# A second stage with twenty chunks instead of twenty-four, and the last four projected inside the delta block

## The chip, the core and the metric

The kernel runs on one NeuronCore of one Trainium2 chip. The time is that of the device for one execution of the program, in microseconds (us). Five engines work side by side, each through its own list of instructions in order: TensorE (PE), VectorE (DVE), ScalarE (ACT), GpSimd (POOL) and SyncE (SP, which here only issues DMAs). They wait for each other through semaphores that the kernel sets by hand. All data is 32-bit floating point. A matmul of that type is recorded twice in the profile, so a group "x2" of one shape is one matmul.

## The reference

One transformer trunk layer over 128 context tokens and 512 latent tokens: layer norm with a modulation, a token mixer of three recurrences (a gated delta rule, a linear recurrent unit, an mLSTM), each gated and projected, and a mixture of experts. What the change touches is cut down here to its core:

```python
def token_mixer(h, p, init_state):
    proj = h @ p['w_in']
    qkv_a, x_b, z_a, beta_a, alpha_a, g_b, q_c, k_c, v_c, o_c, i_c, f_c, gates = _split(proj, IN_SIZES)
    y_a, st_a = delta_mixer(silu(dwconv(qkv_a, p['conv_a'])), z_a, beta_a, alpha_a, ...)
    y_b, st_b = lru_mixer(dwconv(x_b, p['conv_b_w']) + p['conv_b_b'], g_b, p, s_lru)   # (h_f + h_b) * gelu(g_b)
    y_c, st_c = mlstm_mixer(q_c, k_c, v_c, o_c, i_c, f_c, ...)

def gated_delta_chunked(q, k, v, g, beta, s0):          # chunks of 128 tokens, here 5 tiles
    kk = einsum('bnhid,bnhjd->bnhij', kc, kc)
    strict_l = where(strict, bc[..., :, None] * kk * decay, 0.0)
    sol = triangular_solve(eye + strict_l, rhs, left_side=True, lower=True)
    ...                                                  # then a scan over the tiles, forward and backward
    o = rms_norm(o_f + o_b, norm_w) * silu(z)
```

q and k are divided by their norms over the 128 channels of a head before all this. The mod vectors (shift, scale and gate of both halves of the layer) are `silu(c) @ w_mod + b_mod`.

## The kernel before

The program is a row of blocks, each with a list for every engine and a barrier at its end. Two of them are touched.

**`proj1` (lines 400 to 680).** The hidden activations lie transposed in `hT` (8 slices of 128 channels by 640 tokens). The input weights come from memory in ten blocks of 2 MB through `ring`, which holds two. A block has four chunks of 128 output columns; a chunk is 8 slices of one 128x512 and one 128x128 matmul (L464, L465). First come 40 matmuls of 32 columns for the small projections (L442), then 24 chunks in six blocks: the input of the recurrent unit (0 to 3), its gate `g_b` (4 to 7), the delta rule's q, k and v (8 to 19) and its gate z (20 to 23). After each chunk PE does a third of one mod vector: half of its row (L169, `mod_half`, twice), or the turning of a finished row into columns (L176), for which DVE must first have copied the row from `bank[7]` (L654). ACT and DVE take each chunk out of PSUM; chunks of the first and third to fifth block go through a convolution of four steps on DVE (L601 or L608, and L611 three times). Beside chunks 8 to 15 run the gates of the recurrent unit, its two directions are scanned on DVE in one piece each, ahead of chunk 12 and ahead of chunk 16 (`direction`, L643), and GpSimd computes the inner part of gelu after that (L550 to L554). At the end DVE multiplies it out (L675, L677).

**`delta` (lines 798 to 1395).** v and k are turned to tokens by channels (L894, L914), squares (POOL, L1222) are summed by a matmul with ones (L904), ACT makes 1/norm as Ln and Exp (L1141, L1146), DVE multiplies q and k by it (L1262). For each of the five tiles PE forms k k^T (L929) and the decay rows (L920), DVE and ACT make the triangular matrix N (L1275, L1154, L1288). Its 32x32 diagonal blocks go to memory (L807, four DMAs a tile) and come back with one block per partition (L812), where DVE inverts all 80 at once, row by row (L1300, L1303, some 35 us). They go back to memory (L817) and come into place tile by tile (`load_inverse`, 12 DMAs, L831 and L835, which need buffers that POOL has zeroed, L1238). From them PE builds each tile's whole inverse in four products (`inner` L947, `inner_product` L956, `turned` L963, `outer` L971, `outer_product` L980), and a loop of five steps g carries the two directions' states on (L920, L1010, L1017, L1024, L1031, L1037, L1044). Between these PE does projections for the mLSTM, q, k and v, one slice (an eighth of a unit) at a time; the table `FILL` says how many at which place. Then come the four units of the mLSTM's output gate (L1063, `gate_unit`), the sums of squares for the final norm (L1074) and the turning of the mLSTM's k (L1090).

The order of everything is written out by hand: the lists `lab_*` and `l*` number the semaphore steps, and a wait names the step that it wants.

## Time and profile before

| | us |
|---|---|
| time, median of 3 runs (lowest to highest) | 1605.72 (1603.92 to 1609.12) |
| time of the profiled execution | 1603.87 |
| its span from first to last instruction | 1601.9 |
| PE busy | 1364.6 (85% of the span) |
| DVE busy | 579.8 (36%) |
| ACT busy | 279.7 (17%) |
| POOL busy | 106.9 (7%) |
| mean granted TensorE clock | 0.926 of full speed |

The profile is of one execution; 2.0 us of its time lie outside the span. "Idle before" names what ended a wait. A clock of 1.00 is 2.4 GHz, one of 0.50 is 1.2 GHz; a value between them in a stretch is a mixture of the two. `proj1` lasts from 44 to 344 us, the delta block from 344 to 691 us.

### The profile page before, as it was taken

What the parts mean: (1) busy time and instruction counts of PE and PEld (TensorE: products, weight loads), DVE (VectorE), ACT (ScalarE), POOL (GpSimd) and SP (SyncE); (2) the same over time, 40 slices, a digit from 0 to 9 for tenths busy, and PEclk for the clock granted to TensorE, in tenths of its full rate; (3) what the DMA queues carried; (4) which work ended last, traced back from release to release, by engine and by line L of the source; (5) the groups of instructions that cost most, each with busy time, mean ns of one, the idle gap of its engine ahead of it and who ended that gap; (6) DMA issues with size and microseconds to landing.
All of it is one profiled execution on the core that took longest, in us unless ns stands there. A gap on an engine that the chain in (4) does not pass through costs nothing. (4 is left out here: it accounts for less than half of the span.)

```text
span 1601.9 us, 16015 instructions
## 1 busy us (share of the span) xinstructions
PE 1364.6 (85%) x6201; PEld 805.5 (50%) x6201; DVE 579.8 (36%) x1294; ACT 279.7 (17%) x574; POOL 106.9 (7%) x150
## 2 busy tenths in 40 slices
PE   4999995978967999899999999999948888786864
PEld 2655553555635889466777555554543333232321
DVE  4231568223381345244444411115751111110108
ACT  2102441034102433211111100000111101110110
POOL 0000003011000000000000000002011111110100
PEclk9799997989987999999999999999958999998987
DMA  9332322310301101022111127103068999999923
GB/s 374 145 131 106 105 76 82 130 55 1 82 14 32 34 6 58 0 80 66 40 40 40 40 79 246 63 20 141 40 284 325 421 424 423 424 423 373 391 85 151
DMA packets 57742, 242.36 MB, mean 151 GB/s; under 512 B 21668, under 2 KB 30436, under 8 KB 42820
## 3 DMA queue, kind: packets, MB, share of 16 engines
q1 hardware_dynamic: 51476, 229.79, 37.3%
q0 software_dynamic: 6048, 10.50, 1.7%
q8 instruction: 50, 0.82, 0.2%
q10 hardware_dynamic: 144, 1.05, 0.2%
q14 instruction: 24, 0.20, 0.0%
HBM read 233.54 MB, written 19.31 MB: 158 GB/s over the span
## 5 line engine op out<-in xcount | busy, mean ns | idle before, releaser
L464 PE MATMUL bank<-hT,ring 128*128 128x512 f32 x384 | 202.5, 609 | 0.0
L2431 PE MATMUL bank<-ew,xgT 128*64 128x512 f32 x672 | 162.8, 640 | 35.0 <-DMA ew<-in_experts 18.4
L1531 PE MATMUL bank<-hT,w_ab 128*128 128x512 f32 x256 | 131.1, 594 | 0.8 <-issue 0.8
L2431 PEld LDWEIGHTS bank<-ew,xgT 128*64 128x64 f32 x672 | 57.6, 148 | 136.0 <-issue 136.0
L465 PEld LDWEIGHTS bank<-hT,ring 128*128 128x128 f32 x384 | 74.2, 193 | 94.4 <-issue 94.4
L2445 PE MATMUL bank<-ew,hidT 128*64 128x512 f32 x336 | 80.1, 619 | 12.8 <-issue 12.3
L1532 PEld LDWEIGHTS bank<-hT,w_ab 128*128 128x128 f32 x256 | 48.6, 190 | 61.2 <-issue 61.2
L2540 DVE SCALAR_TENSOR_TENSOR uh<-uh,bank 128x256 f32<-128x256 f32 x21 | 8.8, 421 | 191.6 <-ACT uh L2494 191.6
L465 PE MATMUL bank<-hT,ring 128*128 128x128 f32 x384 | 74.6, 276 | 0.0
L1942 PE MATMUL bank<-w_out,mT 128*128 128x512 f32 x160 | 70.9, 604 | 2.2 <-PEq L1464 2.2
L867 PE MATMUL bank<-hT,ring 128*128 128x512 f32 x128 | 66.0, 597 | 0.0
L1646 PE MATMUL bank<-hT,w_c 128*128 128x512 f32 x128 | 65.5, 594 | 0.0
L464 PEld LDWEIGHTS bank<-hT,ring 128*128 128x128 f32 x384 | 59.4, 195 | 9.2 <-issue 3.4
L2445 PEld LDWEIGHTS bank<-ew,hidT 128*64 128x64 f32 x336 | 27.5, 141 | 51.9 <-issue 51.9
L1942 PEld LDWEIGHTS bank<-w_out,mT 128*128 128x128 f32 x160 | 30.8, 194 | 40.3 <-issue 40.3
L1532 PE MATMUL bank<-hT,w_ab 128*128 128x128 f32 x256 | 49.2, 274 | 0.0
L2551 DVE COPY yo<-bank 128x512 f32<-128x512 f32 x21 | 14.5, 692 | 95.3 <-PE bank L2445 95.3
L2494 ACT ACTIVATE uh<-bank 128x256 f32<-128x256 f32 x21 | 8.1, 384 | 184.7 <-PE bank L2431 184.7
L868 PEld LDWEIGHTS bank<-hT,ring 128*128 128x128 f32 x128 | 24.4, 190 | 30.9 <-issue 30.9
L1647 PEld LDWEIGHTS bank<-hT,w_c 128*128 128x128 f32 x128 | 24.3, 190 | 30.6 <-issue 30.6
L1063 PE MATMUL bank<-hT,ring 128*128 128x512 f32 x64 | 34.9, 629 | 5.4 <-ACT og L1215 5.4
L611 DVE SCALAR_TENSOR_TENSOR yc_half<-rawc,cah,yc_half 128x642 f32<-128x642 f32 x36 | 39.1, 1085 | 1.3
(427 smaller groups left out, 2102.6 us busy)
## 6 DMA issues: line engine op xcount, KB each, us to landing
ew<-in_experts SPq DMA_DIRECT2D x41, 2048.0 KB, 20.8
ew<-in_experts SPq DMA_DIRECT2D x41, 1024.0 KB, 22.5
ring<-in_blocks SPq DMA_DIRECT2D x10, 2048.0 KB, 9.5
mhalf<-in_mods SPq DMA_DIRECT2D x16, 1024.0 KB, 5.0
w_ab<-in_merge SPq DMA_DIRECT2D x16, 768.0 KB, 4.4
mstage<-in_mods SPq DMA_DIRECT2D x3, 2048.0 KB, 18.6
w_c<-in_merge SPq DMA_DIRECT2D x8, 768.0 KB, 4.4
yt<-expert_rows SPq DMA_DIRECT2D x5, 1024.0 KB, 9.0
```

What stands on the lines that cost most here:

```text
L464: pe.matmul(lat[:, :], w, hT[:, k, P:T], start=(k == 0), stop=(k == KD - 1))
L465: mm = pe.matmul(ctx[:, 0:P], w, hT[:, k, 0:P], start=(k == 0), stop=(k == KD - 1))
L611: dve.scalar_tensor_tensor(dst, rawc[:, s_, j:j + CW], w[j], dst, ALU.mult, ALU.add).then_inc(v1.step("conv", c, j), 1)
L867: pe.matmul(lat[:, :], w, hT[:, k, P:T], start=(k == 0), stop=(k == KD - 1))
L868: mm = pe.matmul(ctx[:, 0:P], w, hT[:, k, 0:P], start=(k == 0), stop=(k == KD - 1))
L1063: pe.matmul(lat[:, :], w, hT[:, k, P:T], start=(k == 0), stop=(k == KD - 1))
L1531: pe.matmul(bank[5][:, :], w[:, k, :], hT[:, k, P:T], start=(k == 0), stop=(k == KD - 1))
L1532: mm = pe.matmul(bank[7][:, 0:P], w[:, k, :], hT[:, k, 0:P], start=(k == 0), stop=(k == KD - 1))
L1646: pe.matmul(bank[4 * s_][:, :], w_c[x][:, k, :], hT[:, k, P:T], start=(k == 0), stop=(k == KD - 1))
L1942: mm = pe.matmul(bank[2 * (t % 2) + f][:, :], mT[k // 4][:, k % 4, tok(t)], w_out[:, k, 512 * f:512 * f + 512], start=(k == 0), stop=(k == ...
L2431: mm = pe.matmul(bank[2 + x % 2][hs, :], xgT[:, x % 2, k, hs], ew1[:, 2 * (x % 2) + h, 2 * DE * k:2 * DE * (k + 1)], start=(k == 0), stop= ...
L2445: mm = pe.matmul(bank[5 + f][HS * h:HS * h + HS, :], hidT[:, x % 2, P * k + HS * h:P * k + HS * h + HS], ew2[:, 2 * (x % 2) + h, at:at + 5 ...
```

## The change

`proj1` has 20 chunks; the z gate's four become units at the end of the `DENSE` list in the delta block, and their weight block is the ninth to be loaded, not the sixth. The mod work of the four missing chunks is done in chunks 16 to 19, two thirds of a vector each, one of them in the middle of the chunk's sum. Their halves come through two buffers, and ACT, not DVE, copies the last three rows. The scans of a direction are spread, one channel group per chunk (12 to 15 and 16 to 19). The small projections are computed with tokens as columns (16 matmuls) and turned by five transposes after chunk 0. gelu moves to the delta block, to ACT and DVE; GpSimd does none of it. The delta block starts with the keys' norms, whose squares ACT makes at the end of `proj1`; the queries' norms and the turning of v and k come after the five tiles' matrices. The SP queue waits for q's fourth unit only after the blocks are read back, and reads them with two DMAs, not ten. In the loop the decay rows and the key-state product of step g + 1 stand within the building of its inverse.

```diff
-    C1 = 24
+    C1 = 20
+    MOD = {c: ([c] if c < 16 else [2 * c - 16, 2 * c - 15]) for c in range(C1)}
...
-            for t in range(NT):
-                for k in range(KD):
-                    mm = pe.matmul(bank[6][:, 32 * t:32 * t + 32], hT[:, k, tok(t)], w_small[:, k, :],
-                                   start=(k == 0), stop=(k == KD - 1))
+            for k in range(KD):
+                pe.matmul(bank[6][0:32, :], w_small[:, k, :], hT[:, k, P:T], start=(k == 0), stop=(k == KD - 1))
+                mm = pe.matmul(bank[7][0:32, 0:P], w_small[:, k, :], hT[:, k, 0:P], start=(k == 0), stop=(k == KD - 1))
             mm.then_inc(p1.step("small", 0), 1)
...
+                if m < 9:
+                    pe.wait_ge(v1.sem, v1.after("row", m))
+                else:
+                    pe.wait_ge(a1.sem, a1.after("row", m))
+                    if m > 9:
+                        pe.wait_ge(v1.sem, v1.after("column", m - 1))
+                    else:
+                        pe.wait_ge(a1.sem, a1.after("tg1", 7))
+                mod_columns(pe, bank[7 if m < 9 else 6][:, 0:8], mrow[:]).then_inc(p1.step("columns", m), 1)
+            for m in range(5):
...
+                        if k == 3 and len(MOD[c]) == 2:
+                            mod_step(MOD[c][0])
...
+            act.wait_ge(p1.sem, p1.after("small", 0))
+            act.activation(tr[0:32, P:T], bank[6][0:32, :], ACT.Copy).then_inc(a1.step("st", 0), 1)
...
+                if c in (16, 18, 19):
+                    m = {16: 9, 18: 10, 19: 11}[c]
+                    act.wait_ge(used, 2 * (m - 4) + 2)
+                    act.wait_ge(p1.sem, p1.after("columns", m - 1))
+                    act.activation(mrow[:], bank[7][:, :], ACT.Copy).then_inc(a1.step("row", m), 1)
...
-                if c in (12, 16):
-                    direction(0 if c == 12 else 1)
-                if c % 3 == 2:
+                if c % 3 == 2 and c < 16:
                     mod_row(4 + c // 3)
+                if 12 <= c < 20:
+                    scan((c - 12) // 4, c % 4)
                 chunk(c)
-                if c % 3 == 2:
-                    mod_column(4 + c // 3)
+                for i in MOD[c]:
+                    if i % 3 == 2:
+                        mod_column(4 + i // 3)
...
+    DENSE = [("q", j) for j in range(4)] + [("k", j) for j in range(4)] + [("v", t) for t in range(NT)] + [("z", j) for j in range(4)]
+    FILL = {("prep", 1): 8, **{("head", t): 1 for t in range(NT)}, ("sub",): 53}
+    FILL.update({("l0", x): 3 for x in range(4)})
+    FILL.update({("a", 0): 8, ("b", 0): 8, ("c", 0): 10, ("a", 1): 0, ("b", 1): 0, ("c", 1): 8})
+    FILL.update({("a", 2): 4, ("b", 2): 4, ("c", 2): 8, ("a", 3): 4, ("b", 3): 4, ("c", 3): 0, ("a", 4): 0, ("b", 4): 0, ("c", 4): 0})
...
+    lp = [("gcs",)] + [("sum", i) for i in KEYS]
     for t in range(NT):
-        lp += [("kk", t), ("gb", t, 0), ("gb", t, 1)]
+        lp += [("gb", t, 0), ("gb", t, 1), ("kk", t)]
+    lp += [("sum", i) for i in QUERIES] + [(x, t) for x in ("v", "k") for t in range(NT)]
...
-    FILL = {("prep", 0): 4, **{("sum", i): 1 for i in NORMS}, ("prep", 1): 8, **{("head", t): 2 for t in range(NT)}, ("sub",): 46}
-    FILL.update({("l0", x): 3 for x in range(4)})
-    for g in range(NT):
-        FILL.update({(x, g): 2 if g < 2 else 1 for x in "abc"})
-    FILL[("rest",)] = 8 * len(DENSE)
...
-            sp.wait_ge(pd.sem, pd.after("q", 3))
-            load_block(sp, 8)
             for t in range(NT):
                 sp.wait_ge(v3.sem, v3.after("N", t, 1))
...
             sp.wait_ge(n_sent, 16 * 4 * NT)
-            for t in range(NT):
-                for d in range(2):
-                    sp.dma_start((xt if d else xb)[16 * t:16 * t + 16, d, :, :].rearrange("p i j -> p (i j)"),
-                                 n_dram[t, d].rearrange("h r i j -> (h r) (i j)")).then_inc(got_n, 16)
+            for d in range(2):
+                sp.dma_start((xt if d else xb)[0:NB, d, :, :].rearrange("p i j -> p (i j)"),
+                             n_dram[:, d].rearrange("t h r i j -> t (h r) (i j)")).then_inc(got_n, 16)
+            sp.wait_ge(pd.sem, pd.after("q", 3))
+            load_block(sp, 7)
             sp.wait_ge(v3.sem, v3.after("xt"))
             for d in range(2):
                 for dst, src in ((x_dram, xb), (xt_dram, xt)):
...
-            for g in range(2, NT):
+            load_inverse(2)
+            sp.wait_ge(pd.sem, pd.after("v", NT - 1))
+            sp.dma_start(ring[:, 0, :], A["blocks"][8]).then_inc(got_z, 16)
+            for g in range(3, NT):
                 load_inverse(g)
-            sp.wait_ge(pd.sem, pd.after("v", NT - 1))
+            sp.wait_ge(pd.sem, pd.after("z", 3))
             sp.dma_start(ring[:, 0, :], A["blocks"][9]).then_inc(got_o, 16)
...
+                    if kind == "z":
+                        if j:
+                            pe.wait_ge(v3.sem, v3.after("sil", j - 1))
+                        else:
+                            pe.wait_ge(got_z, 16)
+                            pe.wait_ge(ad.sem, ad.after("v", NT - 1))
...
             for t in range(NT):
+                for d in range(2):
+                    if t:
+                        pe.wait_ge(v3.sem, v3.after("A", t - 1, d))
+                    else:
+                        pe.wait_ge(a3.sem, a3.after("ln", KEYS[3], d))
+                    decay_rows(o_bank(d), t, d).then_inc(p3.step("gb", t, d), 1)
+                if t == 0:
+                    fill("prep", 1)
+                    pe.wait_ge(v3.sem, v3.after("norm", 7))
                 if t >= 2:
                     pe.wait_ge(v3.sem, v3.after("N", t - 2, 1))
-                else:
                 for h in range(H):
                     mm = pe.matmul(hd(bank[4 + t % 2], h), kt(t, h), kt(t, h), start=True, stop=True)
                 mm.then_inc(p3.step("kk", t), 1)
-                for d in range(2):
-                    if t:
-                        pe.wait_ge(v3.sem, v3.after("A", t - 1, d))
-                    decay_rows(o_bank(d), t, d).then_inc(p3.step("gb", t, d), 1)
                 fill("head", t)
+            for m, i in enumerate(QUERIES):
+                pe.wait_ge(a3.sem, a3.after("square", i))
+                if m < 2:
+                    pe.wait_ge(v3.sem, v3.after("N", NT - 1, 1))
+                else:
+                    pe.wait_ge(a3.sem, a3.after("ln", QUERIES[m - 2], 1))
+                square_sums(m, i)
+
+            def turn(x, t):
+                for h in range(H):
+                    src = qkv[:, 8 + h, ctok(t)] if x == "v" else kt(t, h)
+                    mm = pe.transpose(bank[4 + t % 4][:, P * h:P * h + P], src, ident)
+                mm.then_inc(p3.step(x, t), 1)
...
             fill("sub")
+            for t in range(NT):
+                if t < 4:
+                    pe.wait_ge(a3.sem, a3.after("v", t if t else 4))
+                else:
+                    pe.wait_ge(a3.sem, a3.after("k", 0))
+                turn("k", t)
...
+            inner(0)
+            fill("l0", 0)
+            inner_product(0)
+            fill("l0", 1)
+            turned(0)
+            gates(0)
+            fill("l0", 2)
+            outer(0)
+            key_state(0)
+            fill("l0", 3)
+            outer_product(0)
+            for g in range(NT):
+                more = g + 1 < NT
+                for d in range(2):
+
+                    if d:
+                        fill("a", g)
...
                 if more:
                     turned(g + 1)
+                    gates(g + 1)
                     outer(g + 1)
+                    key_state(g + 1)
                     outer_product(g + 1)
...
             gate_unit(0)
-            for t in (0, 2, 3):
+            for t in DONE:
                 square_sum(t)
             gate_unit(1)
-            for t in (1, 4):
-                square_sum(t)
             gate_unit(2)
...
+                        dve.wait_ge(ad.sem, ad.after("z", j))
+                        dve.scalar_tensor_tensor(yA[:, j, P:T], yA[:, j, P:T], 1.0, bank[0][:, :], ALU.add, ALU.mult)
+                        dve.scalar_tensor_tensor(yA[:, j, 0:P], yA[:, j, 0:P], 1.0, bank[1][:, 0:P], ALU.add, ALU.mult).then_inc(v3.step("sil", j), 1)
...
                 if more:
+                    weighted(g + 1)
                     put_outer(g + 1)
+                silu_z("c", g)
```

On PE, at the start of the delta block, the rows of before are these, up to the first tile's k k^T (L929) and decay rows (L920); L867 and L868 are slices of the mLSTM's projection and L904 is the sum of squares.

```order
L886 MATMUL bank<-smg,cst 128x20 x2
L887 MATMUL bank<-smg,cst 128x40
L894 MATMUL bank<-cst,qkv 128x128 x20
...
L904 MATMUL bank<-sq,cst 128x321 x2
...
L914 MATMUL bank<-cst,qkv 128x128 x20
L929 MATMUL bank<-qkv 128x128 x4
L920 MATMUL bank<-cst,smg 128x128 x8
```

And now (L951 is the sum of squares, L964 the decay rows, L928 and L929 a slice, L980 is k k^T):

```order
L947 MATMUL bank<-smg,cst 128x20 x2
L948 MATMUL bank<-smg,cst 128x40
L951 MATMUL bank<-xc,cst 128x321 x8
L964 MATMUL bank<-cst,smg 128x128 x8
L928 MATMUL bank<-hT,ring 128x512
L929 MATMUL bank<-hT,ring 128x128
...
L980 MATMUL bank<-qkv 128x128 x4
```

The transposes of v and k have left the place ahead of the first tile, and of sixteen matmuls of squares eight are left there; one whole unit of eight slices stands between, where there were twenty slices.

On the SP queue, before, from the delta block's start to the return of the inverses (L156 is a load of a weight block):

```order
L156 DMA ring<-in_blocks 128x4096
L807 DMA delta_n_blocks<-dl_n 32x8x32 x20
L812 DMA dl_x<-delta_n_blocks 16x1024
L812 DMA dl_xt<-delta_n_blocks 16x1024
...
L817 DMA delta_x_blocks<-dl_x 80x1024
```

And now:

```order
L855 DMA delta_n_blocks<-dl_n 32x8x32 x20
L859 DMA dl_x<-delta_n_blocks 80x1x1024
L859 DMA dl_xt<-delta_n_blocks 80x1x1024
L156 DMA ring<-in_blocks 128x4096
L866 DMA delta_x_blocks<-dl_x 80x1024
```

The twenty sends no longer stand behind the load of a weight block, which waits for PE's fourth unit; the load now stands behind the two reads.

On PE, the second step of the loop, before, from the products that complete its inverse (L980) to the next tile's first product (L947):

```order
L980 MATMUL bank<-dl_f,dl_d_1687 128x64 x4
L980 MATMUL bank<-dl_f,dl_d_1688 128x64 x4
L920 MATMUL bank<-cst,smg 128x128 x8
L1010 MATMUL bank<-dl_s_1685,qkv 128x128 x4
L1010 MATMUL bank<-dl_s_1686,qkv 128x128 x4
L1017 MATMUL bank<-qkv 128x128 x8
L863 MATMUL bank<-ring,hT 128x512 x2
L1024 MATMUL bank<-dl_w_1661,dl_dt_1674 128x128 x4
L1024 MATMUL bank<-dl_w_1662,dl_dt_1675 128x128 x4
L947 MATMUL bank<-dl_dt_1672,dl_n 128x64 x4
```

And now, with L1053 for L980, L964 for L920, L1076 for L1010, L1098 for L1017, L1104 for L1024 and L1020 for L947:

```order
L964 MATMUL bank<-cst,smg 128x128 x8
L1044 MATMUL bank<-dl_dt_1564,dl_n 128x64 x4
L1044 MATMUL bank<-dl_dt_1565,dl_n 128x64 x4
L1076 MATMUL bank<-dl_s_1575,qkv 128x128 x4
L1076 MATMUL bank<-dl_s_1576,qkv 128x128 x4
L1053 MATMUL bank<-dl_f,dl_d_1577 128x64 x4
L1053 MATMUL bank<-dl_f,dl_d_1578 128x64 x4
L1098 MATMUL bank<-qkv 128x128 x8
L1104 MATMUL bank<-dl_w_1551,dl_dt_1564 128x128 x4
L1104 MATMUL bank<-dl_w_1552,dl_dt_1565 128x128 x4
L1020 MATMUL bank<-dl_dt_1562,dl_n 128x64 x4
```

The decay rows and the key-state product have moved ahead of L1053, and no slices are left between it and L1020.

## Rows read from the trace of the kernel before

**Rows 1.** Windows: stretch, its us, busy (x) per engine, PEclk, DMA share, GB/s.
```profile
44.00:691.00 647.00, 573.29 (x2716) 377.70 (x2716) 266.84 (x540) 167.55 (x315) 35.55 (x31) 0.91 0.19 65
...
44.00:61.00 17.00, 16.75 (x81) 16.78 (x81) 1.32 (x4) 1.49 (x2) 0.00 (x0) 0.52 0.63 248
...
272.00:281.00 9.00, 8.40 (x22) 5.21 (x23) 4.86 (x8) 0.74 (x1) 0.00 (x0) 0.55 0.00 0
...
492.00:499.00 7.00, 7.00 (x21) 5.00 (x22) 0.00 (x0) 0.60 (x1) 0.00 (x0) 0.53 0.01 2
...
800.00:1000.00 200.00, 199.21 (x909) 125.50 (x908) 71.56 (x235) 22.49 (x57) 0.00 (x0) 1.00 0.27 87
```

**Rows 2.** PE's timeline, its longest waits: start, us, line [idle before, releaser].
```profile
272.60 1.87 PE L176 MATMUL bank<-cst,mrow 128*128 128x2 f32 x8 [17.52 <-DVE mrow L654]
...
344.07 1.02 PE L886 MATMUL bank<-smg,cst 128*128 128x20 f32 x4 [8.27 <-PEq L414]
...
491.89 3.68 PE L947 MATMUL bank<-dl_dt,dl_n 128*128 128x64 f32 x16 [26.21 <-DMA dl_d<-delta_xt_blocks]
...
667.77 2.08 PE L1063 MATMUL bank<-hT,ring 128*128 128x512 f32 x2 [5.44 <-ACT og L1215]
```

**Rows 3.** PE's timeline, small projections, then two neighbouring slices and a mod half.
```profile
44.25 16.91 PE L442 MATMUL bank<-w_small,hT 128*128 128x32 f32 x80 [3.15 <-PEq L212]
...
67.42 1.02 PE L464 MATMUL bank<-hT,ring 128*128 128x512 f32 x2
...
68.50 1.02 PE L464 MATMUL bank<-hT,ring 128*128 128x512 f32 x2
...
71.84 1.06 PE L169 MATMUL bank<-mhalf,cond 128*32 128x512 f32 x8
```

**Rows 4.** DVE's timeline: one convolution step beside GpSimd's gelu, and without.
```profile
256.00 4.42 DVE L608 TENSOR_SCALAR yc_half<-rawc,cah 128x642 f32<-128x642 f32 x1
...
272.78 0.55 DVE L608 TENSOR_SCALAR yc_half<-rawc,cah 128x642 f32<-128x642 f32 x1
```

**Rows 5.** SP's timeline at the end of `proj1`.
```profile
335.05 0.33 SPq L156 DMA_DIRECT2D ring<-in_blocks  x1
335.50 0.35 SPq L163 DMA_DIRECT2D out_lru<-nlru  x1
```

**Rows 6.** SP's waits over the first 800 us: total, times, longest.
```profile
SPq L414 <- DMA out_lru<-nlru: 7.2, 1, 7.2
```

**Rows 7.** DVE's timeline: last matrix N, first and last step of the inversion.
```profile
419.72 2.15 DVE L1288 SCALAR_TENSOR_TENSOR dl_n<-bank,dl_nb,dl_w 128x128 f32<-128x128 f32 x8
442.85 1.04 DVE L1293 COPY dl_x<-dl_xt 80x1024 f32<-80x1024 f32 x1 [20.97 <-DMA dl_xt<-delta_n_blocks]
...
476.28 2.06 DVE L1307 COPY dl_xt<-dl_x 80x2048 f32<-80x2048 f32 x1
```

**Rows 8.** SP's timeline: the sends of N, and the first inverse's loads.
```profile
421.17 13.57 SPq L807 DMA_DIRECT2D delta_n_blocks<-dl_n  x20
...
484.89 1.74 SPq L831 DMA_DIRECT2D dl_dt<-delta_xt_blocks  x4
```

**Rows 9.** ACT's timeline in the delta block: a whole-gate tanh, a table switch, eight Exps.
```profile
344.05 2.34 ACT L1132 ACTIVATE dl_tz<-yA 128x2560 f32<-128x2560 f32 x1 [6.17 <-PEq L414]
...
370.77 1.28 ACT L1146 ACT_TABLE_LOAD   x1
372.07 5.13 ACT L1146 ACTIVATE rs<-rs 128x642 f32<-128x642 f32 x8
```

**Rows 10.** POOL's timeline, zeroing ahead of the second inverse's loads.
```profile
513.73 0.99 POOL L1238 MEMSET dl_d<- 128x512 f32 x2 [56.84 <-PE bank L980]
```

**Rows 11.** PE's timeline in the loop.
```profile
511.78 1.90 PE L980 MATMUL bank<-dl_f,dl_d 128*128 128x64 f32 x16
...
522.84 2.00 PE L947 MATMUL bank<-dl_dt,dl_n 128*128 128x64 f32 x16 [0.25 <-DMA dl_d<-delta_xt_blocks]
...
539.37 3.47 PE L980 MATMUL bank<-dl_f,dl_d 128*128 128x64 f32 x16 [0.78 <-ACT dl_f L1161]
...
638.52 1.95 PE L1044 MATMUL bank<-dl_qk,dl_u 128*128 128x128 f32 x16
```

390 lines of the change are left out of this document (212 added, 178 removed).

## The prediction, made before the changed kernel had run

> **What bounds the kernel now.** I read the windows first. From 44 to 691 us, the two blocks that change, PE is busy 573.3 of 647 us at a mean granted clock of 0.91, while DVE has 267 us of work and ACT 168 [rows 1]. PE is the only engine that is nearly full, so time goes here in three ways: its work, its idle time (73.7 us), and work done at the low clock. That PE work alone need not slow the clock is seen from 800 to 1000 us, 99.6% busy at 1.00 [rows 1]. The second view is PE's timeline, for the waits. Four make 57.4 us of the 73.7: 17.5 us for DVE's copy of a mod row, 8.3 us at the barrier ahead of the delta block, 26.2 us for the inverse's blocks from memory, and 5.4 us for ACT in the gate units [rows 2]. After each long wait come 4 to 9 us at the low clock: 272 to 281 us at 0.55, 492 to 499 us at 0.53 [rows 1]. Third, the timelines of DVE, ACT, POOL and SP, for what each wait hangs on.
>
> The units of the sum: a slice is 68.50 - 67.42 = 1.08 us, a chunk of eight 8.65, a third of a mod vector about 1.0 [rows 3]. A group of 16 matmuls of 128 or 64 columns in the loop takes some 1.8 us to the next one; 1.9 is recorded [rows 11]. Slices of v have no 128-column part and take 0.87. Below, D is the start of the delta block on PE, 344.07 before [rows 2].
>
> **Small projections.** 16.9 us for 80 records from 44.25 [rows 3], all at the low clock (0.52 with PE busy 16.75 of 17 us [rows 1]): PE had been idle before. Now it is eight pairs of 512 and 128 columns. If their first 4 us are slow, as in the other restarts, that is two pairs of 2.17, six of 1.08, chunk 0 at 8.65 and transposes of 1: 20.5 us, to 64.8. Before, the same point was 71.8, where the first mod half starts [rows 3]. I take -7. Bounds: if the clock stays low until chunk 0, as before, eight pairs of 2.17, two slow slices, six fast ones and the transposes make 29, +1.5; if it never falls, 18.3, -9.
>
> **Scans spread, gelu away from POOL.** Before, DVE does a whole direction ahead of chunk 16's work, then a convolution beside GpSimd: one step takes 4.42 us, which takes 0.55 without it [rows 4]. So the mod row is late and PE waits 17.5. Now a DVE turn is at most a product of 2.8, two scans (1.7), a chunk's convolution (3.6) and a gate's three operations (1.9), near 11 us against a PE turn of 11.9. The wait goes, with the slow 9 us behind it, which did 8.4 x 0.55 = 4.6 us of work in 8.4: -17.5 - 3.8 = -21.3. What is late next: the row copy on ACT at chunk 18. ACT's queue ahead of it is chunk 17's copy, its tanh (after DVE's convolution, some 5 us after the chunk), and two squares of 0.75. That is 7.6 us after chunk 17's end; PE wants it 1 + 4.3 = 5.3 after. +2.4 (bounds 0 and +5).
>
> **Four chunks leave.** -34.6 at this place. They come back below, slice for slice. Mod work is the same.
>
> **The barrier.** DVE's gelu tail goes, but SP loads a block at 335.05, stores the states at 335.50 and waits 7.2 us for them [rows 5, 6]. That stays: PE's wait of 8.3 becomes about 7.5. -0.8. So D comes at 344.1 - 7 - 21.3 + 2.4 - 34.6 - 0.8 = 282.8.
>
> **From D to the first product with an inverse** (491.89 - 344.07 = 147.8 before [rows 2]). Now: sums of the keys' squares, Ln and Exp take 16 us on ACT and DVE, under PE's first unit; the first k k^T is at D + 19. Each tile then costs DVE 4.3 us (two groups of 2.15 [rows 7]) and PE 4.1. N is done at D + 41.6, where it was 421.9 - 344.07 = 77.8 [rows 7]. The sends, 13.57 us for 20, all came after N because SP waited for PE's fourth unit [rows 8]; now four remain, 2.7 us. The merged reads are not in this trace. From the last send, 434.7, to DVE's first step on the blocks, 442.85, it was 8.1 us with five pairs [rows 7, 8]; I take 5, bounds 2 and 12, and they are hidden: DVE is busy with gelu (three operations of 2.8) until D + 52.7, 3 us longer. The inversion takes 35.5 us [rows 7] and comes free at D + 88.
>
> But PE is not there. After the last tile it waits for N (4 us), for ACT between the second and third query sum (3 us: ACT first does gelu's square and tanh, 2.34 each [rows 9]), and for v's first copy; these pieces run at the low clock. The 53 slices begin at D + 60.2, and their first 4 us are slow. POOL zeroes its buffers only after k's last unit, 51 slices on: 60.2 + 2.2 + 55.3 = 117.7; 1.5 for three memsets of 0.5 [rows 10]; then SP's loads, 7.0 from issue to PE's first product (491.89 - 484.89 [rows 2, 8]). The first product is at D + 126. PE's own work reaches it at D + 124.6, so a wait of 26.2 has become 1.6. This rests on PE; the inversion has 28 us in hand.
>
> The switches of ACT's tables stand on this path twice more (Ln, then Exp, for the queries). The trace has 1.28 us from a switch to the first Exp at 372.07, 1.30 after its start [rows 9], and this is in the sum. The Trainium skill (ScalarE: Activation LUTs, "What ACT_TABLE_LOAD costs") adds a drain, 2.66 us in all; by that the two would cost an estimated 2.7 us more.
>
> **The first inverse and the loop.** Before, first inverse's products: 491.9 to 513.7 [rows 2, 11]; now with decay rows and key-state product, 3.6 more, and less of it slow: 24, to D + 150. Then per step, groups of 1.8 and slices: step 0, ten groups and 26 v slices, 43. Step 1: no slices before the next inverse, whose loads are ready 9.1 us after the last product (513.7 to 522.8, of which 1 for POOL's memsets [rows 10, 11]); PE is there after 4.5, so it waits about 4 and gets slow; then z's first unit, whose weights land some 16 us after that same product, just ahead of PE: 36.5. Steps 2 and 3, with 16 and 8 slices of z, each with about 1 us until DVE has emptied the bank: 39.4 and 30.6. Step 4 without slices: 9.5, bound by DVE and ACT as before. In sum 159, so the loop ends at D + 309, against 640.3 - 344.1 = 296.2 [rows 2, 11]: +13, of which 34.6 are the z units, and -21.6 is gain. The waits between L971 and L980, 0.78 each with a slow 3.5 us behind them [rows 11], are covered by the key-state product. z units are not in the trace; bounds for each are 8.65 and 8.65 + 3.
>
> **Gate units.** With all five sums ahead of the second unit, ACT is done with them before the third wants a bank: the 5.4 goes, and the slow 5 us after it (2.4), less 0.5 of waits between the five sums. -7.3.
>
> **Sum**: -7 - 21.3 + 2.4 - 34.6 - 0.8 + 13 - 7.3 = -55.6. Nothing behind 691 us changes; its waits are all on events of its own blocks. From the profiled execution (1603.87) this is 1548.3, from the median, 1.85 higher, 1550.1. I say 1550.
>
> **Rivals.**
> - *The gain is smaller, since the stretch of short matmuls falls to the low clock.* With the slices gathered in groups of 8 and 26, step 4, most of step 1 and the stretch from D + 37 to D + 60 have none. The trace shows such a fall beside short matmuls with small waits (L980 at 3.47 where it is 1.90 [rows 11]). Some 25 us more at the low clock cost 12: 1562. For it: the places. Against it: two of them are in my sum as slow already.
> - *More gain*: the clock stays up in the small projections and the loads of step 1 are as quick as the other steps': 1541.
> - *The inverse's chain still decides.* If the merged reads or the gelu ahead of the inversion cost over 28 us more, the wait at the first product comes back. 28 us on a chain whose pieces are all in the trace but one is too much; 1560 to 1575.
> - *Slower.* The granted clock stays at 1.2 GHz through the whole delta block, because the wide matmuls are in fewer, longer groups. Each us there costs a half, so it must be low for 120 us more of the 350 before the gain of 55.6 is gone and 5 more lost: 1612. Against it: the clock came back within 9 us of the restarts at 272 and 492 us [rows 1].
> - *The change does not do what it says*: DVE's turn at chunks 12 to 19 is longer than PE's 11.9 and the wait comes back in pieces, 2 us a chunk: 1566.
>
> **How the numbers follow.** My forecast has 0.55 (1543 to 1557 its own range), the short-matmul rival 0.18, more gain 0.10, the chain 0.06, the DVE rival 0.05, slower 0.04, and 0.02 for no change. The range of 8 in 10 is 1539 to 1568; the bounds above (small projections -2 to +8.5, the row copy -2.4 to +2.6, z units up to +12) lie within it together when they go different ways. 0.3% of the time is 4.8 us, about what a measurement of this kernel can tell from none: faster 0.94, same 0.02, slower 0.04.
>
> **What would show each step.** Small projections: the first mod half starts near 65. Scans: no PE wait over 3 us before the barrier, and no DVE convolution step over 1.1. Barrier: PE's wait there 7 to 8, named by SP's store, D near 283. Delta block: N done near D + 42, the first product near D + 126 after a wait under 3. Loop: one wait of some 4 us, in step 1, its end near D + 309. Gate units: no wait over 1 us. I am wrong if D comes after 290, if the first product comes after D + 135, or if the block's end is not near 635.

## The result, and the profile after

The changed kernel takes 1549.07 us (median of 4 runs, 1546.01 to 1550.23) against 1605.67 beside it (4 runs): a ratio of 0.9632, with a 95% interval of 0.9602 to 0.9662. The forecast was 1550, with a range of 1539 to 1568. The profiled execution took 1550.23 us with a span of 1548.5; before it was 1603.87 and 1601.9.

First the windows, those that answer to [rows 1]; the columns are the same.

```profile
44.00:634.00 590.00, 557.15 (x2673) 356.42 (x2673) 254.54 (x540) 182.02 (x342) 9.98 (x20) 0.96 0.21 71
...
283.00:342.00 59.00, 48.16 (x230) 34.62 (x230) 39.24 (x108) 32.62 (x50) 1.10 (x3) 0.83 0.11 23
...
800.00:1000.00 200.00, 199.21 (x813) 117.33 (x812) 52.76 (x169) 18.42 (x45) 0.00 (x0) 1.00 0.30 97
```

The two blocks now end near 634 us where they ended at 691. PE's work in them is 557.2 us (573.3 before), at a granted clock of 0.96 (0.91), and its idle time has fallen from 73.7 to 32.8 us. The weakest stretch left is 283 to 342 us, the matrices N: 48.2 of 59 us busy at 0.83. From 800 to 1000 us PE is full at 1.00, as before.

Next PE's timeline, with its longest waits and the two matmul groups that begin and end the delta block. It answers to [rows 2].

```profile
257.89 1.05 PE L176 MATMUL bank<-cst,mrow 128*128 128x2 f32 x8 [1.09 <-ACT mrow L545]
...
282.70 1.01 PE L947 MATMUL bank<-smg,cst 128*128 128x20 f32 x4 [7.49 <-PEq L419]
...
324.10 4.62 PE L951 MATMUL bank<-xc,cst 128*128 128x321 f32 x8 [4.05 <-DVE dl_n L1382]
331.45 2.48 PE L951 MATMUL bank<-xc,cst 128*128 128x321 f32 x4 [2.74 <-ACT xc L1220]
...
341.52 0.66 PE L994 MATMUL bank<-cst,qkv 128*128 128x128 f32 x4 [3.29 <-ACT v_tm L1253]
...
405.77 3.68 PE L1020 MATMUL bank<-dl_dt,dl_n 128*128 128x64 f32 x16 [4.52 <-DMA dl_d<-delta_xt_blocks]
...
481.68 3.68 PE L1020 MATMUL bank<-dl_dt,dl_n 128*128 128x64 f32 x16 [4.11 <-DMA dl_d<-delta_xt_blocks]
485.15 3.73 PE L1111 MATMUL bank<-dl_qd,dl_s 128*128 128x128 f32 x16
...
589.40 1.95 PE L1124 MATMUL bank<-dl_qk,dl_u 128*128 128x128 f32 x16
...
599.84 4.96 PE L1156 MATMUL bank<-dl_osq,cst 128*128 128x512 f32 x10
...
635.47 0.30 PE L1665 MATMUL bank<-cst,modc 128*64 128x128 f32 x1 [1.40 <-DVE modc L1847]
```

The wait of 17.52 us for the mod row is 1.09 us. The barrier's is 7.49 (8.27 before), and D, the start of the delta block, is 282.70. The 26.21 us for the inverse's blocks are 4.52, a second wait of 4.11 has come in step 1, and the group behind each takes 3.68 for 1.90, with the next one in step 1 at 3.73 for 2.00; the granted clock is 0.50 in both stretches, the level of 1.2 GHz. The five sums of squares (599.84) run on without a wait, and so do the gate units around them. The next block starts at 635.47, where it was 692.46.

The small projections, to set beside [rows 3]:

```profile
45.95 1.88 PE L455 MATMUL bank<-hT,w_small 128*32 128x512 f32 x2 [3.15 <-PEq L212]
...
50.13 1.02 PE L455 MATMUL bank<-hT,w_small 128*32 128x512 f32 x2
...
65.96 1.06 PE L169 MATMUL bank<-mhalf,cond 128*32 128x512 f32 x8
```

Two pairs at the low clock (0.50 from 46 to 50.1 us, 1.00 behind that), then 1.02 a wide matmul: the first mod half comes 20.0 us after the first projection, where it took 71.84 - 44.25 = 27.6.

Last, in the order of time, DVE's first and last operation of the inversion, and SP's sends, merged reads and loads of the first inverse. They answer to [rows 7] and [rows 8].

```profile
335.33 1.05 DVE L1393 COPY dl_x<-dl_xt 80x1024 f32<-80x1024 f32 x1 [0.56 <-DMA dl_xt<-delta_n_blocks]
...
368.77 2.18 DVE L1407 COPY dl_xt<-dl_x 80x2048 f32<-80x2048 f32 x1
```

```profile
309.51 16.25 SPq L855 DMA_DIRECT2D delta_n_blocks<-dl_n  x20
327.00 0.93 SPq L859 DMA_DIRECT2D dl_x<-delta_n_blocks  x1
327.98 0.71 SPq L859 DMA_DIRECT2D dl_xt<-delta_n_blocks  x1
...
398.95 1.76 SPq L880 DMA_DIRECT2D dl_dt<-delta_xt_blocks  x4
...
403.59 0.91 SPq L884 DMA_DIRECT2D dl_d<-delta_xt_blocks  x2
```

The inversion is over at 371.0, but POOL zeroes the buffers at 397 and SP issues the first load at 399, when k's last unit is done: the inversion's end had 28 us in hand, as forecast. SP needs 5.5 us to issue the twelve transfers of one inverse, and PE goes on 1.3 us after the last is issued.

**Where the 53.4 us of the span came from.** The blocks end 57.0 us earlier on the chip's clock, though the first projection starts 1.7 us later (45.95, was 44.25); behind the block 3.6 us are given back. Both lie in code that the change leaves alone. The first is for the most part one group of 16 matmuls ahead of the first stage, which took 1.92 us in one profile and 3.64 in the other. It is not the change's doing: the long form also stands in b_spread and b_nopool, which have the old first stage, and the short one in four of the nine edits of the changed kernel below. PE's timeline of before, then of after:

```profile
25.38 1.92 PE L169 MATMUL bank<-mstage,cond 128*32 128x512 f32 x16 [1.17 <-DMA mstage<-in_mods]
```

```profile
25.07 3.64 PE L169 MATMUL bank<-mstage,cond 128*32 128x512 f32 x16 [1.18 <-DMA mstage<-in_mods]
```

Of the other 3.6 us, 2.7 lie in the experts' part: from its first transpose to its last it took 329.7 us before, 332.4 in this profile, and 329.3 in the second profile of the same kernel (a_same below). What makes these 3 us stays open.

### The profile page after: what moved, and what is told of

Its sections match the earlier page's. It is cut to its first block and busy times, and to the rows that moved or that the text cites. A ratio compares the mean times of both kernels' runs of the same rounds, so it can differ in the third digit from the quotient of the medians.

```text
span 1548.5 us, 15938 instructions
## 1 busy us (share of the span) xinstructions
PE 1353.8 (87%) x6158; PEld 787.8 (51%) x6158; DVE 565.8 (37%) x1291; ACT 292.6 (19%) x597; POOL 81.3 (5%) x139
## 5 line engine op out<-in xcount | busy, mean ns | idle before, releaser
L2547 PE MATMUL bank<-ew,xgT 128*64 128x512 f32 x672 | 163.3, 642 | 35.5 <-DMA ew<-in_experts 19.0
L501 PE MATMUL bank<-hT,ring 128*128 128x512 f32 x320 | 165.3, 598 | 0.0
L928 PE MATMUL bank<-hT,ring 128*128 128x512 f32 x192 | 98.6, 595 | 2.2 <-DVE yA L1445 2.2
L502 PEld LDWEIGHTS bank<-hT,ring 128*128 128x128 f32 x320 | 60.8, 190 | 76.5 <-issue 76.5
L1648 PEld LDWEIGHTS bank<-hT,w_ab 128*128 128x128 f32 x256 | 48.7, 190 | 61.2 <-issue 61.2
L502 PE MATMUL bank<-hT,ring 128*128 128x128 f32 x320 | 61.5, 274 | 0.0
L929 PEld LDWEIGHTS bank<-hT,ring 128*128 128x128 f32 x192 | 36.5, 190 | 45.9 <-issue 45.9
L501 PEld LDWEIGHTS bank<-hT,ring 128*128 128x128 f32 x320 | 48.5, 192 | 9.4 <-issue 5.2
L2058 PEld LDWEIGHTS bank<-w_out,mT 128*128 128x128 f32 x160 | 30.7, 194 | 40.3 <-issue 39.8
L2667 DVE COPY yo<-bank 128x512 f32<-128x512 f32 x21 | 14.5, 691 | 96.8 <-PE bank L2561 96.8
L2524 PE MATMUL bank<-cst,xg 128*128 128x128 f32 x168 | 24.7, 293 | 18.1 <-DMA xg<-h_rows,ig 11.8
L1763 PEld LDWEIGHTS bank<-hT,w_c 128*128 128x128 f32 x128 | 24.3, 190 | 30.6 <-issue 30.6
L1647 PEld LDWEIGHTS bank<-hT,w_ab 128*128 128x128 f32 x256 | 38.9, 192 | 1.0 <-issue 1.0
## 6 DMA issues: line engine op xcount, KB each, us to landing
ew<-in_experts SPq DMA_DIRECT2D x41, 1024.0 KB, 21.3
```

Of the source, the lines that this page charges most:

```text
L501: pe.matmul(lat[:, :], w, hT[:, k, P:T], start=(k == 0), stop=(k == KD - 1))
L502: mm = pe.matmul(ctx[:, 0:P], w, hT[:, k, 0:P], start=(k == 0), stop=(k == KD - 1))
L928: pe.matmul(lat[:, :], w, hT[:, k, P:T], start=(k == 0), stop=(k == KD - 1))
L929: mm = pe.matmul(ctx[:, 0:P], w, hT[:, k, 0:P], start=(k == 0), stop=(k == KD - 1))
L1647: pe.matmul(bank[5][:, :], w[:, k, :], hT[:, k, P:T], start=(k == 0), stop=(k == KD - 1))
L1648: mm = pe.matmul(bank[7][:, 0:P], w[:, k, :], hT[:, k, 0:P], start=(k == 0), stop=(k == KD - 1))
```

## The experiments

Times are medians of the runs made beside runs of the kernel before on the same chip. Since executions differ by 1 to 3 us ahead of the first stage and in the experts' part, I read each effect from the trace too, as the distance from D to the next block's first matmul (352.8 us in the changed kernel) or from the first projection to D (236.8).

**The changed kernel again** (a_same), with no edit, for comparison with the others.

> The changed kernel again, unchanged, beside the others of this chip: 1549, ratio 0.963. It is what they are compared with.

Measured: 1547.90 (1546.95 to 1548.53, 5 runs), ratio 0.9642 [0.9628, 0.9655]; from D on 352.7.

**Scans spread alone, on the kernel before** (b_spread).

```diff
-                if c in (12, 16):
-                    direction(0 if c == 12 else 1)
                 if c % 3 == 2:
                     mod_row(4 + c // 3)
+                if 12 <= c < 20:
+                    scan((c - 12) // 4, c % 4)
```

> The kernel before with the scans alone spread, two a chunk over chunks 12 to 19; gelu's three products stay on GpSimd behind the last scan. Mine (two causes, each enough for a wait of its own): the wait of 17.5 us at chunk 17 goes, but the products (16 us on GpSimd) now run beside chunk 19's convolution, which takes 14 us there where it took 3.3; the row copy at chunk 20 is then some 17 us behind chunk 19 and PE, which wants it 10 behind, waits 6 to 7 us. Gain 9 to 13, so about 1594. Rival (the lump of eight scans was all of it): no wait over 3 us before the barrier, gain 19 to 21, 1585. Rival (GpSimd was all of it): the full 17 us wait again at chunk 20, no gain.

Measured: 1594.72 (6 runs), ratio 0.9933 [0.9912, 0.9954]. The wait has moved from chunk 17 to chunk 20 and is 7.29 us. DVE's convolution beside GpSimd's three products, on DVE, POOL and PE:

```profile
276.18 4.22 DVE L608 TENSOR_SCALAR yc_half<-rawc,cah 128x642 f32<-128x642 f32 x1 [0.24 <-DVE rawc L595]
280.43 9.87 DVE L611 SCALAR_TENSOR_TENSOR yc_half<-rawc,cah,yc_half 128x642 f32<-128x642 f32 x3
```

```profile
272.99 7.06 POOL L550 TENSOR_TENSOR G<-yB 128x2560 f32<-128x2560 f32 x1 [272.53 <-DVE Q L643]
280.13 2.45 POOL L552 TENSOR_SCALAR G<-G 128x2560 f32<-128x2560 f32 x1
282.66 6.03 POOL L554 TENSOR_TENSOR G<-G,yB 128x2560 f32<-128x2560 f32 x1
```

```profile
292.59 1.87 PE L176 MATMUL bank<-cst,mrow 128*128 128x2 f32 x8 [7.29 <-DVE mrow L655]
```

**GpSimd's products left out, scans in one piece** (b_nopool).

```diff
-            pool.tensor_tensor(G4[:], yB[:], yB[:], ALU.mult).then_inc(g1.step("g", 0), 1)
...
-            act.wait_ge(g1.sem, g1.after("g", 2))
-            act.activation(G4[:], G4[:], ACT.Tanh, scale=math.sqrt(2.0 / math.pi))
+            act.wait_ge(v1.sem, v1.after("scan", 1, 3, 1))
+            act.activation(G4[:], yB[:], ACT.Tanh, scale=math.sqrt(2.0 / math.pi))
```

> The kernel before with the scans in one piece, and without gelu's three products on GpSimd (they are left out, the tanh is taken of the plain value, so the output is another). Mine: chunk 16's convolution takes 0.55 + 2.7 us instead of 4.4 + 9.9, the row copy comes 11 us earlier and PE's wait falls from 17.5 to some 6.5; gain 11 to 13, about 1594. Rival (lump alone): the wait stays at 17, 1605. Rival (GpSimd alone): no wait over 3 us, gain 21, 1585.

Measured: 1596.82 (9 runs), ratio 0.9934 [0.991, 0.9957]. The wait for the mod row:

```profile
262.69 1.87 PE L176 MATMUL bank<-cst,mrow 128*128 128x2 f32 x8 [6.54 <-DVE mrow L641]
```

So there were two causes, and each leaves a wait of some 7 us when the other is gone. From the first projection to D the kernel before takes 299.8 us, with the scans spread 288.5, without the products 287.4: gains of 11.3 and 12.4. The change does both, and is worth 20.0 there (236.8, with 34.6 for the four chunks, 7.6 for the projections and 0.8 for the barrier taken out), or 21.1 without the 1.1 that the row copy on ACT costs. Each cause is about half of the wait, and the two gains nearly add.

**The old form of the small projections** (a_small_old).

```diff
-            for k in range(KD):
-                pe.matmul(bank[6][0:32, :], w_small[:, k, :], hT[:, k, P:T], start=(k == 0), stop=(k == KD - 1))
-                mm = pe.matmul(bank[7][0:32, 0:P], w_small[:, k, :], hT[:, k, 0:P], start=(k == 0), stop=(k == KD - 1))
+            for t in range(NT):
+                for k in range(KD):
+                    mm = pe.matmul(bank[6][:, 32 * t:32 * t + 32], hT[:, k, tok(t)], w_small[:, k, :],
+                                   start=(k == 0), stop=(k == KD - 1))
...
-                    if c == 0:
...
-                        for t in range(NT):
-                            mm = pe.transpose(bank[6][:, 32 * t:32 * t + 32], tr[0:32, tok(t)], ident[0:32, 0:32])
```

> The changed kernel with the small projections in their old form, 80 matmuls of 32 columns. Mine: the first mod half starts 7 us later, nothing behind it takes this up, so +7: ratio to before 0.9675, about 1556. Rival (PE is on no path in the first stage, the loads or DVE are): 0 to 2.

Measured: 1556.24 (5 runs), ratio 0.9699 [0.9673, 0.9726].

```profile
43.66 17.06 PE L456 MATMUL bank<-w_small,hT 128*128 128x32 f32 x80 [3.15 <-PEq L212]
...
71.24 1.06 PE L169 MATMUL bank<-mhalf,cond 128*32 128x512 f32 x8
```

The first mod half is 27.6 us after the first projection instead of 20.0, and D comes 7.8 us later by the same measure. Nothing behind takes it up.

**The states' store ahead of the weight load** (a_store_first).

```diff
+                if c == C1 - 1:
+                    sp.wait_ge(got_lev, 16)
+                    sp.wait_ge(v1.sem, v1.after("state", 1))
+                    store(sp, O["lru"], nlru[:])
                 if c % 4 == 3:
                     sp.wait_ge(p1.sem, p1.after("chunk", c))
                     load_block(sp, c // 4 + 2)
             sp.wait_ge(used, 16)
-            sp.wait_ge(got_lev, 16)
-            sp.wait_ge(v1.sem, v1.after("state", 1))
-            store(sp, O["lru"], nlru[:])
```

> The changed kernel with the store of the scans' states sent before the load of the next weight block, not behind it. Mine: the store lands some 4 us earlier, the barrier then waits for DVE's last operations (they end at 280.2 in the trace, where PE is done at 275.2 and goes on at 282.7): wait 5.4 where it was 7.5, gain 2, ratio 0.962. Rival (the store alone makes the wait): wait of 2 or less, gain 6 and a shorter slow stretch, ratio 0.959.

Measured: 1545.15 (5 runs), ratio 0.9621 [0.9595, 0.9647]. SP's and PE's timelines:

```profile
270.77 0.35 SPq L163 DMA_DIRECT2D out_lru<-nlru  x1
274.35 0.33 SPq L156 DMA_DIRECT2D ring<-in_blocks  x1
```

```profile
280.48 1.01 PE L948 MATMUL bank<-smg,cst 128*128 128x20 f32 x4 [5.37 <-PEq L419]
```

The wait is 5.37, as forecast: the store's 7 us decide by 2 only, then DVE's end does. The time alone would not tell 2 us from none.

**Diagonal blocks sent late again** (a_send_late).

```diff
+            sp.wait_ge(pd.sem, pd.after("q", 3))
             for t in range(NT):
                 sp.wait_ge(v3.sem, v3.after("N", t, 1))
```

> The changed kernel with SP waiting for the fourth query unit before it sends the first diagonal blocks, as before the change; all else as changed. Mine: the blocks go out from D + 82 (D is the start of the delta block on PE), 13.6 us for twenty, the reads take 9.6 as the changed kernel's trace shows, the inversion 35.5, its stores and loads 12: the first product comes near D + 153 where it is D + 123, PE waits some 30 us, about 1577. So the early sends are what took the inverse off the path, with some 28 us in hand. Rival (the key norms alone freed it, sends at either time are early enough): 1549. Rival (the 28 us in hand are not there): over 1590.

Measured: 1576.76 (4 runs), ratio 0.9827 [0.9809, 0.9845]. PE in its timeline:

```profile
425.36 1.12 PE L995 MATMUL bank<-cst,qkv 128*128 128x128 f32 x4 [25.31 <-ACT k_tm L1259]
435.19 3.67 PE L1021 MATMUL bank<-dl_dt,dl_n 128*128 128x64 f32 x16 [8.71 <-DMA dl_d<-delta_xt_blocks]
```

The first product is at D + 153.2 and waits of 25.3 and 8.7 us stand ahead of it; the part from D on is 381.3 us long, 28.6 more. The early sends took the inverse off the path. They need the early matrices N as well, which were not put back alone: before, the last N was done at D + 77.8, and my estimate from the rows (2.7 for its sends, 9.6 for the reads, 35.5 for the inversion, 13.5 from its end to the first product, as in this run) puts the first product at D + 139 then. The inversion starts 51.6 us later in D's time and the first product comes 30.1 later, so the slack is 21.5 us: the 28 in hand at the inversion's end include some 6.5 for its blocks to be stored (here it ends at 421.7, and the first load is issued at 428.3), which I had not taken off. In detail the sum was less good than its total: twenty sends took 9.7 us (13.6 taken), and from the last send to the blocks' arrival it was 14.5 (9.6 taken), with a 2 MB load issued right behind the reads.

**Ten reads instead of two** (a_ten_reads).

```diff
-            for d in range(2):
-                sp.dma_start((xt if d else xb)[0:NB, d, :, :].rearrange("p i j -> p (i j)"),
-                             n_dram[:, d].rearrange("t h r i j -> t (h r) (i j)")).then_inc(got_n, 16)
+            for t in range(NT):
+                for d in range(2):
+                    sp.dma_start((xt if d else xb)[16 * t:16 * t + 16, d, :, :].rearrange("p i j -> p (i j)"),
+                                 n_dram[t, d].rearrange("h r i j -> (h r) (i j)")).then_inc(got_n, 16)
...
-            dve.wait_ge(got_n, 32)
+            dve.wait_ge(got_n, 32 * NT)
```

> The changed kernel with ten reads of the diagonal blocks where two merged ones stand. Mine: the inversion starts behind gelu's operations on DVE in either form (two reads: DVE waited 0.6 us for them; five pairs took 8.1 us behind the last send before, two take 9.6) and its end has 28 us in hand: no change, 1548, and DVE's wait ahead of the inversion under 1 us. Rival (ten reads are much slower to issue and land): DVE waits 3 us or more, the time still unchanged. Rival (the inversion's end is on the path): +3 or more.

Measured: 1548.50 (4 runs), ratio 0.962 [0.9598, 0.9642]. DVE's timeline:

```profile
334.11 1.05 DVE L1394 COPY dl_x<-dl_xt 80x1024 f32<-80x1024 f32 x1
```

DVE does not wait for the ten at all (D + 52.0; with two it waited 0.56 in the changed kernel's profile and 1.09 in the other). So merging the reads gains nothing; they land 9.6 us behind the last send, the ten at most 8.9, and the difference is hidden here.

**The z units cut out of the loop but for their last slice** (a_no_z). Seven eighths of the z gate's product are left out, so the kernel computes other values.

```diff
                     for k in range(KD):
+                        if kind == "z" and k < KD - 1:
+                            yield
+                            continue
...
+                            one = kind == "z" or k == 0
...
```

> The changed kernel with the four z units of the loop cut to their last pair of matmuls each (seven eighths of the z gate's product are left out, so the output is another). Mine (the units stand in PE's time, but they also cover waits for the inverse's loads that then come back, 4 us and a slow group in steps 2 and 3): of 30 us of matmuls 17 to 20 are saved, about 1531. Rival (a unit in the loop costs its full 8.65): 30 to 32 saved, 1518. Rival (the loop hides them, as its steps are bound by DVE, ACT and loads): under 8 saved, over 1541.

Measured: 1516.13 (4 runs), ratio 0.9438 [0.9424, 0.9453]. By the time this is the rival. But the time is no measure here: with other values the router sends the tokens elsewhere. The experts' part has 20 tiles instead of 21; from the next block's first matmul to the end of the span it takes 898.2 us, 910.0 in a_same. Behind D 337.6 us are left of 352.7: the slices were worth 15.2 us. In the loop, PE's last products of inverses 1 to 4, and two waits that came back:

```profile
470.11 1.90 PE L1057 MATMUL bank<-dl_f,dl_d 128*128 128x64 f32 x16
...
500.48 1.90 PE L1057 MATMUL bank<-dl_f,dl_d 128*128 128x64 f32 x16
...
511.84 3.68 PE L1024 MATMUL bank<-dl_dt,dl_n 128*128 128x64 f32 x16 [4.65 <-DMA dl_d<-delta_xt_blocks]
...
533.51 1.90 PE L1057 MATMUL bank<-dl_f,dl_d 128*128 128x64 f32 x16
...
543.28 3.67 PE L1024 MATMUL bank<-dl_dt,dl_n 128*128 128x64 f32 x16 [3.06 <-DMA dl_d<-delta_xt_blocks]
...
563.23 1.90 PE L1057 MATMUL bank<-dl_f,dl_d 128*128 128x64 f32 x16
```

Steps 1 to 3 take 30.4, 33.0 and 29.7 us where they took 38.0, 39.6 and 30.7. Seven slices in step 1 cost 7.6 us, fourteen in step 2 cost 6.6, and seven in step 3 one. Half of the 30.2 us of slices removed comes back as waits of 4.65 and 3.06 for loads, with slow groups of 3.7 behind them. My mechanism stands, with 15 in place of 17 to 20 (I had counted one slow group behind each wait that comes back, and there are two), and both rivals fall.

**Decay rows and key-state products late again** (a_late_keys).

```diff
                     turned(g + 1)
-                    gates(g + 1)
                     outer(g + 1)
-                    key_state(g + 1)
                     outer_product(g + 1)
+                    gates(g + 1)
+                    key_state(g + 1)
...
                 if more:
+                    put_outer(g + 1)
                     weighted(g + 1)
-                    put_outer(g + 1)
```

> The changed kernel with decay rows and key-state products behind the inverse's last product again (and DVE's weighting behind its copy), as before the change. Mine: between that product and the two ahead of it nothing covers ACT's copies: waits of 0.25 and 0.78 us in each of four steps and a group at the low clock behind them (3.5 for 1.9), 2.3 a step, +8 to +10, about 1557. Rival (waits under 1 us cost nothing but themselves): +4. Rival (the slices in the step had covered them anyway): 0.

Measured: 1556.24 (5 runs), ratio 0.9683 [0.9663, 0.9702]; from D on 361.2, 8.5 more. PE's timeline in the first step:

```profile
465.05 2.00 PE L1044 MATMUL bank<-dl_dt,dl_n 128*128 128x64 f32 x16 [0.30 <-ACT dl_d L1268]
467.83 3.57 PE L1053 MATMUL bank<-dl_f,dl_d 128*128 128x64 f32 x16 [0.78 <-ACT dl_f L1263]
...
482.21 1.97 PE L1020 MATMUL bank<-dl_dt,dl_n 128*128 128x64 f32 x16 [1.95 <-DVE dl_qk L1469]
```

The waits of 0.30 and 0.78 with a slow 3.57 behind them are there again; in the other three steps the waits come back too, but the group behind them takes 2.45, 1.97 and 2.81, so that "a group at the low clock" in each step was too much. One part of the account was missed: the moved groups now stand ahead of the next inverse, so that the 4.1 us for its loads are gone, and 1.95 us for DVE come in their place. Where no such wait falls away, the order should cost more than 8.5; no run shows that.

**Two sums of squares behind the second gate unit again** (a_rms_old).

```diff
-            for t in DONE:
+            for t in (0, 2, 3):
                 square_sum(t)
             gate_unit(1)
+            for t in (1, 4):
+                square_sum(t)
             gate_unit(2)
```

> The changed kernel with the two last sums of squares behind the second gate unit again, as before the change. Mine: ACT then cannot turn to its Exp and to the gate's tanh before them, PE's wait of 5.4 us ahead of the third unit is back with the slow stretch behind it: +7.3, about 1555, ratio to before 0.969. Rival (the z gate's part on DVE and ACT has moved into the loop, so the wait does not come back): 0 to 1.

Measured: 1555.49 (5 runs), ratio 0.967 [0.9652, 0.9687]; from D on 360.2, 7.4 more. PE's waits from 280 to 660 us (line, releaser: total, times, longest) have the old one again, to the tenth:

```profile
PE bank L1145 <- ACT og L1318: 5.4, 1, 5.4
```

**The inverse's loads in two parts** (a_split).

```diff
             def load_inverse(g):
-                if g:
-                    sp.wait_ge(g3.sem, g3.after("d", g, 1))
-                else:
-                    sp.wait_ge(g3.sem, g3.after("dt", 1, 1))
+                sp.wait_ge(g3.sem, g3.after("dt", g, 1))
                 for d in range(2):
...
                         sp.dma_start(heads(dt_[g % 2][d][:])[b, :, b], src).then_inc(got_d[g % 2], 16)
+                sp.wait_ge(g3.sem, g3.after("d", g, 1))
+                for d in range(2):
+                    t = tile_of(g, d)
                     for r in ((1, 3) if d else (0, 2)):
```

> The changed kernel with each inverse's loads in two parts: the eight into the tiles as soon as these are zeroed, and only the four into the diagonal copy behind its own zeroing. Mine (PE's two waits of 4.5 and 4.1 us for these loads are SP's time to issue twelve of them behind GpSimd's zeroing, 5.5 us, not the landing): four are issued in 1.8 us and land 2 later, the waits fall to about 0.5 and 1, and the slow products behind them to 2: gain 7 to 11, ratio about 0.957, 1540. Rival (the landing of the transfers decides): both waits stay above 3, gain under 2.

Measured: 1539.59 (5 runs), ratio 0.9592 [0.9576, 0.9608]; from D on 343.6, 9.1 less. SP's timeline for the first inverse, and PE's:

```profile
375.93 1.75 SPq L877 DMA_DIRECT2D dl_dt<-delta_xt_blocks  x4
377.73 1.85 SPq L877 DMA_DIRECT2D dl_dt<-delta_x_blocks  x4
395.69 0.78 SPq L884 DMA_DIRECT2D dl_d<-delta_x_blocks  x2
```

```profile
398.81 1.96 PE L1020 MATMUL bank<-dl_dt,dl_n 128*128 128x64 f32 x16
...
405.29 3.40 PE L1029 MATMUL bank<-dl_f,dl_d 128*128 128x64 f32 x16 [1.89 <-ACT dl_f L1263]
...
474.45 1.97 PE L1020 MATMUL bank<-dl_dt,dl_n 128*128 128x64 f32 x16 [1.34 <-DVE dl_qk L1469]
```

Eight loads go out at 376, under the units, and four behind the zeroing. The first product has no wait at all; 1.89 us for ACT's copy are next. In step 1 the load is no longer what comes last, but DVE's product with the decay (1.34).

**Both gains together** (a_best): the edits of a_store_first and a_split, of each the line that matters.

```diff
+                if c == C1 - 1:
...
+                    store(sp, O["lru"], nlru[:])
...
+                sp.wait_ge(g3.sem, g3.after("dt", g, 1))
...
+                sp.wait_ge(g3.sem, g3.after("d", g, 1))
```

> The changed kernel with both edits that gained: the store of the states ahead of the weight load, and the inverse's loads in two parts. They are at two places of the chain and should add: -8.3 and -2.1, about 1537.5, ratio 0.958. Rival (with D earlier, another event of the delta block is late and takes part of it back): 1539 to 1542.

Measured: 1535.00 (median of all 6 runs, ratio 0.9537 [0.9518, 0.9556]); five lie between 1531.94 and 1536.75, and one took 4905.52 us, of which I have no trace and no explanation; the ratio leaves it out. From the first projection to the next block it is 577.6 us long, 11.7 less than a_same: 2 at the barrier (the wait is 5.4) and 9.4 behind D. They add. It is the fastest version of this study, 0.989 of the changed kernel by the two ratios.

## Why the prediction was right, step by step

| step | forecast | trace |
|---|---|---|
| small projections | -7 | -7.6 |
| scans, GpSimd, row copy on ACT | -21.3 + 2.4 | -20.0 (what the other terms leave), of it +1.1 for the row copy |
| four chunks | -34.6 | 4 x 8.65, a slice being 1.08 as before |
| barrier | -0.8, wait 7.5 | -0.8, wait 7.49 |
| D | 282.8 | 282.70 |
| N done | D + 41.6 | D + 41.3 |
| waits between | 4, 3, and v's copy | 4.05, 2.74, 3.29 |
| slices begin | D + 60.2 | D + 59.3 |
| inversion free | D + 88 | D + 88.3 |
| first product | D + 126, wait 1.6 | D + 123.1, wait 4.52 |
| first inverse done | D + 150 | D + 148.1 |
| steps 0 to 4 | 43, 36.5, 39.4, 30.6, 9.5 | 42.8, 38.0, 39.6, 30.7, 9.4 |
| loop ends | D + 309 | D + 308.7 |
| gate units | -7.3 | -7.9 |
| block's end | 635 | 635.47 |

D at 282.70 is partly luck: the projections started 1.7 us later than before, so that the first stage gained 1.8 us more than the sum said. Of these 1.8, 1.3 are in the row copy on ACT, which cost 1.1 instead of 2.4, and 0.6 in the small projections; the scans' own part came to 21.1 for 21.3. The parts that the prediction lists for a DVE turn (2.8, 1.7, 3.6 and 1.9) make 10.0 and not "near 11"; nothing hangs on it, since no wait above 1.1 us is left ahead of the barrier.

Three steps were mis-sized. *The merged reads* took 9.6 us from the last send, not 5, near the upper bound of 12; gelu hid all but 0.6 of it, so the price was nothing, as the working said, but the reason to merge them is not there (a_ten_reads). *The first product*: "PE's own work reaches it at D + 124.6, so a wait of 26.2 has become 1.6". PE was there at D + 118.6: the slices began 0.9 earlier and not at the low clock (2.2), and the twenty transposes behind them took 2.35 us where the sum left 5. POOL and SP hang on k's last unit, so the product came only 3 us earlier, and the wait grew to 4.52. What decides there is the issue of twelve loads (a_split). *Step 1* was 38.0 for 36.5, though its wait was 4.11, as forecast: three groups behind it were slow (3.68, 3.73 and 2.77 us), 4.3 us more than at the full clock. The prediction says only that PE "gets slow" there and gives no price, so which part of the 36.5 was short stays open.

The two switches of ACT's tables for the queries took 1.30 us each, from 329.07 to the Ln at 330.36 and from 337.07 to the Exp at 338.37, and each began as the operation before it ended: the 2.7 us more that the prediction set beside its sum as an estimate did not come.

That the inverse's chain would not decide was the term that could have cost most, and the sends' part of it is shown by putting it back: 28.6 us (a_send_late). The order in the loop and the gate units are each shown alone, at 8.5 and 7.4 us, and the scans' term splits into two causes of about equal size. The order of the norms ahead of the matrices N, without which the sends could not be early, is not shown alone. Of the rivals, the short matmuls at the low clock did not show outside the places in the sum: the granted clock is 0.96 over both blocks. DVE's turns gave no wait in pieces, and the clock did not stay up in the small projections. Not tried: gelu back on GpSimd in the changed kernel, and the row copies back on DVE.

## What to carry to other kernels

A wait can have two causes: either alone gained 11 to 12 us here and left 7 of the 17.5, and only both took it away (21 us). So a term for "the wait goes" must ask what each edit leaves by itself. When a wait for a transfer disappears, look at what now sits closest behind the event: here the issue of twelve transfers behind one zeroing that eight of them did not need, and 9 us were to be had by giving the eight their own condition. And where the values steer later work, as in a router, an experiment that changes them is read from the trace of its own block, never from the total.
